# Feed-forward up projection: 512-column operand and one set of PSUM banks

## The reference, cut to what matters

```python
def conv_glu_ffn(h, w_up, conv_w, conv_b, w_down):
    u = causal_depthwise_conv(h @ w_up, conv_w) + conv_b
    gate, up = jnp.split(u, 2, axis=-1)
    return (jax.nn.gelu(gate, approximate=True) * up) @ w_down
```

## Time and profile before

| | us |
|---|---|
| median of 3 runs (lowest, highest) | 978.39 (978.35, 978.64) |
| the profiled execution, whole | 978.03 |
| its span (first to last instruction) | 976.0 |
| PE busy | 961.9 (99%) |
| DVE busy | 663.4 (68%) |
| ACT busy | 500.4 (51%) |
| stage ffn, first matmul of its first unit to the last of its last down unit | 179.40 to 367.34 |

### The profile page before, as it was taken

One profiled execution on the slowest core, in us unless ns is written; L12 is line 12 of the kernel. 1 busy time (PEld: TensorE's weight loads), 2 busy tenths in 40 slices (PEclk: granted clock), 3 DMA queues, 4 the chain that ended last, 5 costly groups with the idle time before them and its releaser, 6 DMA issues.

```text
span 976.0 us, 15567 instructions
## 1 busy us (share of the span) xinstructions
PE 961.9 (99%) x6269; PEld 874.1 (90%) x6269; DVE 663.4 (68%) x838; ACT 500.4 (51%) x664; POOL 34.8 (4%) x48
## 2 busy tenths in 40 slices
PE   8999999999999999999999999999999999999997
PEld 8999998999999998999998888888899888888885
DVE  5766757787777787587658765666767676655564
ACT  5855663664554547444346444434655464443442
POOL 2000001200000000010000000001010000000000
PEclk9999999999999999999999999999999999999999
DMA  9942222566555545555555565655465347565641
GB/s 296 259 130 87 87 65 91 169 209 209 174 206 172 204 147 167 174 173 173 173 173 183 181 205 181 206 177 189 123 163 173 122 135 240 173 200 187 201 143 44
DMA packets 128898, 165.08 MB, mean 169 GB/s; under 512 B 20911, under 2 KB 111468, under 8 KB 128716
## 3 DMA queue, kind: packets, MB, share of 16 engines
q1 hardware_dynamic: 127227, 159.31, 50.9%
q0 software_dynamic: 1312, 4.68, 1.6%
q10 hardware_dynamic: 304, 0.33, 0.1%
HBM read 163.26 MB, written 1.05 MB: 168 GB/s over the span
## 4 chain that ended last, share of the span: by engine, by line
PE 95%; DVE 2%; ACT 1%; issue 1%; DMA 0%; POOL 0%; POOLq 0%; DVEq 0%; ACTq 0%
PE ps L270 23%; PE ps L272 22%; PE ps L271 22%; PE ps L854 11%; PE ps L851 6%; PE ps L1972 2%; PE ps L1351 2%; PE ps L1372 1%; PE ps L1967 1%; PE ps L1238 1%; PE ps L532 1%; PE ps L1361 0%; PE ps L2101 0%; DMA X<-in_x_dram 0%; PE ps L2121 0%
## 5 line engine op out<-in xcount | busy, mean ns | idle before, releaser
L233 DVE TENSOR_TENSOR w_lo<-raw,w_hi 128x2048 fp32r<-128x2048 f32 x147 | 334.3, 2276 | 133.7 <-ACT w_hi L219 133.7
L219 ACT ACTIVATE w_hi<-raw 128x2048 fp32r<-128x2048 f32 x147 | 279.9, 1904 | 129.7 <-PE ps L272 128.4
L270 PE MATMUL ps<-hT,w_hi 128*128 128x256 f32 x712 | 203.7, 286 | 1.4 <-DVE hT L491 0.9
L271 PE MATMUL ps<-hT,w_lo 128*128 128x256 f32 x712 | 201.4, 283 | 0.0
L272 PE MATMUL ps<-hT,w_hi 128*128 128x256 f32 x712 | 201.4, 283 | 0.0
L270 PE MATMUL ps<-w_hi,act_hi 128*128 128x512 f32 x416 | 163.0, 392 | 0.0
L272 PE MATMUL ps<-w_lo,act_hi 128*128 128x512 f32 x416 | 162.0, 389 | 0.0
L271 PE MATMUL ps<-w_hi,act_lo 128*128 128x512 f32 x416 | 162.0, 389 | 0.0
L854 PE MATMUL ps<-hT,w_hi 128*128 128x512 f32 x480 | 150.8, 395 | 0.0
L270 PEld LDWEIGHTS ps<-hT,w_hi 128*128 128x128 f32 x712 | 136.4, 192 | 2.8 <-issue 1.5
L271 PEld LDWEIGHTS ps<-hT,w_lo 128*128 128x128 f32 x712 | 136.5, 192 | 0.6
(11 more groups left out here) (325 smaller groups left out, 1102.9 us busy)
## 6 DMA issues: line engine op xcount, KB each, us to landing
raw<-in_mlp_w_dram SPq DMA_DIRECT2D x64, 1024.0 KB, 5.4
raw<-in_w_up_dram SPq DMA_DIRECT2D x22, 1024.0 KB, 5.1
raw<-in_a_w_in_dram SPq DMA_DIRECT2D x16, 1024.0 KB, 5.5
raw<-in_w_in_dram SPq DMA_DIRECT2D x11, 1024.0 KB, 6.6
raw<-in_w_down_dram SPq DMA_DIRECT2D x11, 1024.0 KB, 5.0
raw<-in_a_w_out_dram SPq DMA_DIRECT2D x8, 1024.0 KB, 4.9
raw<-in_w_out_dram SPq DMA_DIRECT2D x4, 1024.0 KB, 4.9
raw<-in_b_w_o_dram SPq DMA_DIRECT2D x4, 1024.0 KB, 4.9
```

The costliest lines, as they stand in the source:

```text
L219: nc.scalar.activation(w_hi[:, s, 0:n], raw[:, r, 0:n], ACT.Copy).then_inc(hi_ready, 1)
L233: nc.vector.tensor_tensor(w_lo[:, s, 0:n], raw[:, r, 0:n], w_hi[:, s, 0:n].bitcast(F32), ALU.subtract).then_inc(lo_ready, 1)
L270: nc.tensor.matmul(o, a[0], b[0], start=start, stop=False, skip_group_check=shared)
L271: nc.tensor.matmul(o, a[1], b[0], start=False, stop=False, skip_group_check=shared)
```

## The change

18 of the 22 up-projection units, those of pairs 1 to 9, use `up_halves` in place of `up`; pairs 0 and 10 keep `up` or its like. A unit then needs two banks (gate: 0 and 1, up: 2 and 3), and every pair uses the same four. So the gate unit of pair j waits for the gate product of pair j-1 (`f.r >= 2j-1`), its up unit for the up product of pair j-1 (`f.r >= 2j`), and pair 1, whose gate unit overwrites the banks of both units of pair 0, waits for both products of pair 0 (`f.r >= 2`). ACT copies the right halves out (counted by the new `f.e`), DVE adds the left halves into `scaled` and then multiplies from there.

```diff
@@ ffn_pe, step
-                pe.wait_ge(lo_ready, u + 1 + i * PERIOD)
-                if not one:
-                    pe.wait_ge(f.r, j * 2 - 2)
-                up(W[2 * m], u)
-                pe.wait_ge(lo_ready, u + 2 + i * PERIOD)
-                up(W[2 * m + 1], u + 1)
+                last = isinstance(j, int) and j == f.pairs - 1
+                for half in range(2):
+                    pe.wait_ge(lo_ready, u + half + 1 + i * PERIOD)
+                    pe.wait_ge(f.r, 2 if one else j * 2 + (half - 1))
+                    if last:
+                        up(W[2 * half], u + half)
+                    else:
+                        up_halves(2 * half, u + half)
@@ ffn_act, step
                 for half in range(2):
+                    if not first:
+                        act.wait_ge(unit_used, u + half + 1 + i * PERIOD)
+                        act.wait_ge(f.f, j)
+                        nc.scalar.copy(tiles2(act_tmp, 2 * m + half), banks[:, 2 * half:2 * half + 2, S:2 * S]).then_inc(f.e, 1)
                     split_hi(act, u + half + 3, i)
                     act.wait_ge(f.r, j * 2 + (half + 1))
-                    if not first and half == 0:
-                        act.wait_ge(f.f, j)
@@ ffn_dve, step
-                    dve.wait_ge(unit_used, u + half + 1 + i * PERIOD)
-                    nc.vector.tensor_tensor(tiles2(scaled, 2 * m + half), W[2 * m + half][:].rearrange("p (t s) -> p t s", t=PAIR),
+                    if first:
+                        dve.wait_ge(unit_used, u + half + 1 + i * PERIOD)
+                        z = W[half][:].rearrange("p (t s) -> p t s", t=PAIR)
+                    else:
+                        dve.wait_ge(f.e, j * 2 + (half - 1))
+                        z = tiles2(scaled, 2 * m + half)
+                        nc.vector.tensor_tensor(z, banks[:, 2 * half:2 * half + 2, 0:S], tiles2(act_tmp, 2 * m + half), ALU.add).then_inc(f.z, 1)
+                        dve.wait_ge(f.z, j * 2 + (half - 1))
+                    nc.vector.tensor_tensor(tiles2(scaled, 2 * m + half), z,
                                             rrow.unsqueeze(1).to_broadcast([P, PAIR, S]), ALU.mult).then_inc(f.r, 1)
@@ ffn_dve, ending
-                                                W[2 * m + half][:, c].rearrange("p (t s) -> p t s", t=n),
+                                                W[2 * half][:, c].rearrange("p (t s) -> p t s", t=n),
```

More of the change, by code:

```diff
@@ L738, in __init__ @@
                     self.r = sem("ffn_r")
+                    self.e = sem("ffn_e")
+                    self.z = pair_z
                 else:
@@ L742, in __init__ @@
                     self.z = pair_z
-                    self.zbase = sum(f.pairs - 1 for n, f in before.items() if n != "gmlp")
+                    self.zbase = 2 * (FT1 // PAIR - 2) + sum(f.pairs - 1 for n, f in before.items() if n != "gmlp")
         def each_pair(eng, f, per, step, u_of, ending=None):
@@ L843, in mlp_sync @@
             load(sp, f.u0 + 2 * f.pairs - 1)
[L846 to L856, removed]
         def mlp_pe(pe, f, n):
@@ L930, in mlp_dve, with up_halves @@
             each_pair(dve, f, 6, step, lambda j: f.u0 + 2 * j - 1)
+        def up_halves(b, u):
+            w_h, w_l = weights(u, KT)
+            for k in range(KT):
+                for t in range(PAIR):
+                    nc.tensor.matmul(banks[:, b + t, S:2 * S], w_l[:, k, t * P:(t + 1) * P], hT[:, k, 0, :], start=k == 0, stop=False,
+                                     skip_group_check=True)
+                for t in range(PAIR):
+                    mm = nc.tensor.matmul(banks[:, b + t, :], w_h[:, k, t * P:(t + 1) * P], hT[:, k, :, :].rearrange("p x s -> p (x s)"),
+                                          start=False, stop=k == KT - 1, skip_group_check=True)
+            mm.then_inc(unit_used, 1)
         def conv_taps(j, half, t, tap):
```

## The result

| | before | after |
|---|---|---|
| median, us (lowest, highest; 13 runs each, side by side) | 978.36 (978.03, 978.64) | 980.43 (980.00, 981.88) |
| profiled execution / its span, us | 978.03 / 976.0 | 981.17 / 979.2 |
| mean granted clock in the span | 0.999 | 0.995 |
| PE, DVE, ACT busy, us | 961.9, 663.4, 500.4 | 962.7, 675.9, 509.7 |

The ratio is 1.0024, 95% interval 1.0017 to 1.0031: slower by 2.1 us, where 979.1 was forecast. Of the 13 runs after, nine took 980.00 to 980.46 us and four 981.17 to 981.88; the profiled one is of the four. All 13 have a mean clock of 0.995 to 0.997; the 13 runs before lie within 0.6 us of each other.

The account below looks back on a forecast made before the run. The prediction took TensorE's instruction stream as the bound: -3.6 us saved, 0 for added work, +4.3 us for pair 1's wait gave 978.7 us, or 979.1 as a median. Range with the clock's fall: 978.3 to 981.6 us.

Parts of the forecast that it names:

- The term gained: Pairs 1 to 9 on PE: the new form takes 16.58 us per pair, 0.40 us less, saving 3.6 us.
- The work added on ACT and DVE: 18 copies (10.6 us on ACT) and 18 additions (12.4 us on DVE) cost PE 0; bound 1.8 us.
- the layout: Timetable of one pair's new order on ACT and DVE from a gate unit's end; smallest slack before PE needs data 4.7 us.
- The term lost: Pair 1 waits for both products of pair 0: PE starts 4.2 us late, loses 4.3 us, idle some 4.1 us.
- the fourth rival: Pair 1's wait costs nothing if pair 0's up product directly follows its unit: 975.9 us at most, 974.8 at best; chance 0.03.
- small loss, clock holds: The forecast itself: saving 3.6 us, pair 1's wait 4.3 us, full clock kept, 979.1 us; chance 0.58.
- the rival in which the clock falls in the new gap: At pair 1's wait: slow matmuls afterwards cost 1.6 us, giving 980.7 us, up to 982.3; chance 0.33.

Follow-up runs that it names:

- banks exchanged: Changed kernel with gate units in banks 2 and 3, up units in 0 and 1, so pair 1's gate unit waits for nothing: 974.67 us, ratio 0.996.
- extra additions of 512 columns: Changed kernel with bank pairs swapped, plus one unread 512-column addition beside each of the 18 additions on DVE: 979.87 us, ratio 1.0016.
- 16 warm-up matmuls: Changed kernel with 16 identity-by-identity matmuls into a bank nobody reads, ahead of pair 1: 979.03 us, ratio 1.0007.
- the wait alone: Kernel before, old unit form, with only pair 1 made to wait for both products of pair 0: 984.13 us, ratio 1.006.
- the early product and 8 warm-ups: Changed kernel with pair 0's up product ahead of the gate half's four taps on DVE, plus 8 unneeded matmuls in the remaining gap: 977.51 us.
- 8 warm-up matmuls: Changed kernel with 8 identity-by-identity matmuls into a bank nobody reads, ahead of pair 1: 979.31 us, in two groups.

## Why the prediction was right in its three terms and wrong on the clock

**The term gained: right.** Forecast 16.58 us per pair and 3.6 us in all; the trace has 16.59, and the version in which nothing else changes (banks exchanged) is 3.7 us below the median before (3.9 below the 978.55 beside it), and its stage is 3.56 us shorter. The estimate of 0.7 us that follows from the small fixed part in the Trainium skill ("TensorE: Matmul & The Clock Gate", section "Wait — 56ns, not 53.3ns?") is excluded by this difference.

**The work added on ACT and DVE: right.** It costs PE nothing, and in the changed kernel the layout fits. DVE (line 1028, line 233) and PE (line 270):

```profile
205.09 0.69 DVE L1028 TENSOR_TENSOR union<-ps,act_tmp 128x512 f32<-128x512 f32 x1 [2.81 <-ACT act_tmp L978]
...
252.83 2.29 DVE L233 TENSOR_TENSOR w_lo<-raw,w_hi 128x2048 fp32r<-128x2048 f32 x1 [1.12 <-ACT w_hi L219]
```

```profile
259.62 0.39 PE L270 MATMUL ps<-w_hi,act_hi 128*128 128x512 f32 x1
```

The wait of PE lets DVE catch up: it stands idle for 2.81 us ahead of pair 1's first addition. A third `split_lo` of a pair ends at 252.83 + 2.29 = 255.12, 4.5 us before the down unit that needs it (the layout has 4.7). In the kernel with exchanged banks PE doesn't wait, DVE enters pair 1 late, and the layout's premise that DVE begins each pair on time fails:

```profile
216.02 2.29 DVE L233 TENSOR_TENSOR w_lo<-raw,w_hi 128x2048 fp32r<-128x2048 f32 x1 [1.13 <-ACT w_hi L219]
```

```profile
219.86 0.39 PE L270 MATMUL ps<-w_hi,act_hi 128*128 128x512 f32 x1
```

There the same `split_lo` ends at 216.02 + 2.29 = 218.31, so the slack is only 1.55 us (219.86 - 218.31), and what counts is how much DVE has to spare in each pair, 0.8 us. With the extra additions of 512 columns, 0.94 us more per pair, it paid 3.2 us of wait, well inside the 4.7 us of the layout.

**The term lost: right.** Forecast a start 4.2 us late after 4.1 us of idle time; measured 4.21 and 4.06. Put alone into the kernel before it costs 5.6 to 5.8 us, wait and clock together, and without it the changed form is faster than both kernels. The "product right behind its unit" of the fourth rival was priced at 975.9 at most; built, it gives 975.99.

**The clock: the step that failed.** The forecast gave 0.58 to "small loss, clock holds" and 0.33 to the rival in which the clock falls in the new gap. The rival happened: the profile shows the fall, and the other 12 runs are all slower than the slowest with 16 warm-up matmuls (980.00 against 979.20 us). It came at about the price given for it: 980.7 was its time, 980.43 came. The number lies in the stated range (978.3 to 981.6) because that range took the rival in; the terms of the likeliest case alone gave 978.6 to 979.6, and 980.43 is also just beyond the 980.35 up to which the prediction would call it no change. What failed is the weighing. One fall, 4.9 us after a last matmul, was set against a gap of 4.1 us. The prediction itself said that one fall is no bound, and still held the clock that stays up to be the likelier; here the clock fell 1.9 us after the last matmul, and with gaps of 2.3 to 2.5 us in 5 of 11 runs each. The rule of the Trainium skill ("TensorE: Matmul & The Clock Gate", section "Why this matters for your kernels": an idle gap of this size between bursts brings the lower clock) was named as the rival's and given too little: the trace after agrees with it.

The price is in part luck. The 1.6 us was read from the matmuls at the start of the span, where the slow clock was inferred from their spacing alone: the profile's clock reads 1.00 there (window 2 to 4 us of the kernel before). 1.4 us is measured in the median and 2.2 us in the profiled execution, whose slow stretch is longer; the rival's "up to 982.3" covers that.

**What stays open.** Why nine runs take 980.0 to 980.5 and four 981.2 to 981.9. The one profiled, of the four, has the slow clock over 194.4 to 201.2 us, of which PE lost 2.2. In the kernel with the wait alone the runs split in the same way, and there the profiled one is of the faster three: its slow stretch lasted from 196.9 to 200.3. That the nine have such a shorter stretch fits this and their mean clock of 0.996 or 0.997 against 0.995, but none of them was profiled. What decides in one execution whether the clock falls in a gap of 2.3 to 3.2 us isn't shown either. Also not shown is what the single run at 979.02 with the early product and 8 warm-ups met; among the 85 runs of the kernel before there was one like it (979.98, mean clock 0.996).

## What to carry to other kernels

When every pass of a loop shares one set of buffers, look at the first pass apart from the steady ones: which buffers it writes first can decide the sign (974.67 against 980.43 us here, with the same instructions but for bank numbers and one wait). An idle gap of TensorE can have a price beyond its length, the slow clock: here it was met in about half the runs at 2.3 to 2.5 us, and in all at 4.06 us. If the gap can't be removed, matmuls nobody needs, together shorter than it, take that part away (16 of them in a gap of 4.2 us). Where another engine enters the loop late, whether work added on it is covered is told by its time for one iteration while it is catching up, against TensorE's.

## What the runs showed of the hardware that was not expected

- The clock can fall after PE has resumed: with the wait alone PE resumed at 196.29 us and slowed at 196.9; with 8 warm-up matmuls it resumed at 196.60 and slowed at about 197.3 (clock 0.82 over 196 to 198). In the changed kernel the clock had fallen at 194.4, before PE resumed at 196.47.
- The same program with the same gap (2.3 or 2.5 us) has a faster and a slower group of executions, about half each and 1.7 to 1.8 us apart, and a profile of the slower one shows the fall. A gap of 3.2 us passed without a fall in one profiled execution.
- An fp32 matmul of identity by identity, 128 columns, is two instructions in the trace: 16 in the program are 32 there, and they take 3.7 us (30 take 6.9).
- A DVE addition of 64 columns between two dependent DVE instructions is free: a dependent instruction starts 0.72 us after the start of a 512-column addition and an independent one 0.60 us after it, and the small one fits into the difference.
